# Five reorderings inside a two-block transformer kernel on one core: router work between memory-key tiles, orders in three attentions, last norm by token

## The reference, cut to what matters

```
block 1: h = x + mix(stick_breaking_attention(8 heads of 64), retention(8 heads, values of 128))
         h = h + hierarchical_moe(rms_norm(h))       # 16 experts, 2 per token, router by group
         x = rms_norm(h)
block 2: x = x + heads @ w_out,  heads = sparse latent attention (8 heads) ++ dilated attention (8 heads)
         x = x + cross_attention(rmsnorm(x), rmsnorm(mem))   # 4 heads of 256, 256 memory tokens
         x = x + square(relu(rmsnorm(x) @ w_up)) @ w_down
return rmsnorm(x)
```

## Time and profile before

| | us |
|---|---|
| median of 3 runs (lowest, highest) | 1667.63 (1666.0, 1667.67) |
| the profiled execution's own time | 1664.19 |
| its span, first to last instruction | 1662.4 |
| PE busy in the span | 1621.7 |
| mean granted TensorE clock | 0.995 |

### The profile page before, as it was taken

The page is one execution under the profiler, slowest core; times in us unless marked ns, Lnnn a source line. Parts: engine busy times, 40 slices in busy tenths (PEclk is TensorE's granted clock), DMA queues, the critical chain, the costliest instruction groups (busy, mean ns, idle before and its releaser), DMA issues.

```text
span 1662.4 us, 21089 instructions
## 1 busy us (share of the span) xinstructions
PE 1621.7 (98%) x7972; PEld 1318.5 (79%) x7972; DVE 924.4 (56%) x1116; ACT 733.0 (44%) x880; POOL 605.3 (36%) x253
## 2 busy tenths in 40 slices
PE   9999999999999999999999999999999999999996
PEld 7988888588887888888898668667877888888885
DVE  6244210682465799898967689893433552232313
ACT  5345222334344788878853332674333322221221
POOL 1412264134342243222313645663422444344441
PEclk9999999999999999999999999999999999999998
DMA  5211153212235999999954314101321222222221
GB/s 195 102 52 51 38 152 114 79 73 101 101 107 178 396 421 406 390 392 395 376 228 146 101 63 154 67 1 48 132 74 51 79 98 101 101 101 89 95 95 51
DMA packets 47139, 249.25 MB, mean 150 GB/s; under 512 B 9472, under 2 KB 10240, under 8 KB 20704
## 3 DMA queue, kind: packets, MB, share of 16 engines
q1 hardware_dynamic: 40880, 235.75, 38.2%
q0 software_dynamic: 5184, 8.40, 1.3%
q10 hardware_dynamic: 1008, 4.19, 0.6%
HBM read 236.05 MB, written 16.78 MB: 152 GB/s over the span
## 4 chain that ended last, share of the span: by engine, by line
PE 77%; issue 11%; DVE 6%; POOL 3%; ACT 2%; DMA 1%; SPq 0%; POOLq 0%; DVEq 0%; ACTq 0%
PE psum L229 22%; PE psum L231 21%; PE psum L230 21%; POOL w_lo L148 3%; PE psum L2208 2%; DVE kept_bias L2075 1%; DVE top L2074 1%; PE psum L662 1%; PE psum L2243 1%; PE psum L2231 1%; PE psum L1244 1%; PE psum L2479 1%; PE psum L681 1%; DMA raw<-in_w_dense 1%; PE psum L2499 1%
## 5 line engine op out<-in xcount | busy, mean ns | idle before, releaser
L148 POOL TENSOR_TENSOR w_lo<-raw,w_hi 128x2048 fp32r<-128x2048 f32 x91 | 419.2, 4606 | 701.6 <-ACT w_hi L142 663.3
L142 ACT ACTIVATE w_hi<-raw 128x2048 fp32r<-128x2048 f32 x96 | 183.4, 1910 | 313.8 <-PE psum L231 313.8
L229 PE MATMUL psum<-x_hi,w_hi 128*128 128x512 f32 x808 | 316.5, 392 | 1.4 <-POOL w_lo L148 0.7
L230 PE MATMUL psum<-x_lo,w_hi 128*128 128x512 f32 x808 | 314.4, 389 | 0.0
L231 PE MATMUL psum<-x_hi,w_lo 128*128 128x512 f32 x808 | 314.4, 389 | 0.0
L1262 DVE TENSOR_TENSOR moe_lo<-moe_w,moe_hi 128x2048 fp32r<-128x2048 f32 x100 | 227.7, 2290 | 31.0 <-ACT moe_hi L1252 29.9
L1252 ACT ACTIVATE moe_hi<-moe_w 128x2048 fp32r<-128x2048 f32 x100 | 190.9, 1915 | 30.1 <-PE psum L231 17.8
L229 PEld LDWEIGHTS psum<-x_hi,w_hi 128*128 128x128 f32 x808 | 151.7, 188 | 35.0 <-issue 2.0
L230 PEld LDWEIGHTS psum<-x_lo,w_hi 128*128 128x128 f32 x808 | 151.7, 188 | 31.7 <-issue 0.7
L231 PEld LDWEIGHTS psum<-x_hi,w_lo 128*128 128x128 f32 x808 | 151.7, 188 | 31.7
L434 DVE TENSOR_TENSOR res<-res,psum 128x512 f32<-128x512 f32 x56 | 38.4, 687 | 214.4 <-PE psum L231 214.4
(11 more groups left out here) (377 smaller groups left out, 2914.7 us busy)
## 6 DMA issues: line engine op xcount, KB each, us to landing
raw<-in_w_dense SPq DMA_DIRECT2D x96, 1024.0 KB, 4.8
moe_w<-in_w_moe_ahead SPq DMA_DIRECT2D x54, 1024.0 KB, 14.3
moe_w<-in_w_moe SPq DMA_DIRECT2D x48, 1024.0 KB
yrow<-expert_rows SPq DMA_DIRECT2D x8, 512.0 KB, 7.9
res<-in_x SPq DMA_DIRECT2D x4, 512.0 KB, 6.4
decay<-in_decay SPq DMA_DIRECT2D x8, 256.0 KB, 5.0
hn_rows<-hn_tok ACTq DMA_DIRECT2D x4, 512.0 KB, 7.8
out<-res SPq DMA_DIRECT2D x4, 512.0 KB, 2.7
```

What stands on the lines that cost most here:

```text
L142: act.activation(w_hi[c % RING][:, :], raw[c % RING][:, :], ACT.Copy).then_inc(hi_ready, 1)
L148: pool.tensor_tensor(w_lo[c % RING][:, :], raw[c % RING][:, :], w_hi[c % RING][:, :].bitcast(F32), ALU.subtract).then_inc(lo_ready, 1)
L229: pe.matmul(out, lh, rh, start=first, stop=False)
L230: pe.matmul(out, lh, rl, start=False, stop=False)
```

## The change

- Stick-breaking: the second `ret_v` tile of a head goes to bank 6 and waits for the low half of the last pair's values instead of the copy of the first tile; a pair's values wait until that tile is copied. On VectorE, softplus of head 0 stands before `size(1)`, and `logs_low(0)` before the copy of tile 2.
- Router: `rows(2)` stands behind tile 0 of `k_mem`, the ranks behind tile 1, `rows(3)` and the lists behind tile 2. Before, ranks, `rows(2)` and `rows(3)` stood behind tile 1 and the lists behind tile 2.
- Attention: the bias of the dilated heads is loaded before the chunks of `v_b`'s stage; the first exponential of head 0 and its table load stand between the copies of `v_b`; one chunk of the layer `out2` is rounded behind the exponentials of head 1 and subtracted by GpSimd behind all heads; VectorE normalises head 0 before it takes head 1.
- Cross attention: head 3 is turned into banks 4 and 5, right behind head 2; then come the values of both. VectorE normalises head 3 before the low halves of head 1.
- Last norm: sums of squares are made per token, as columns of 4; root and reciprocal are on 128 x 4; the reciprocal is widened by a copy and turned by 4 transposes into bank 5, and the eight products read it there. The sum of the first seven squares is reduced while the eighth is made.

```diff
@@ stick-breaking
+    SECOND_V = [tiles_of(h)[1] for h in range(HEADS) if TILES_V[h] == 2]
-            if j >= 1:
-                pe.wait_ge(bank_free, V_T + j + 4)
+            if j in SECOND_V:
+                pe.wait_ge(bank_free, V_T + j + 3)
+            elif j >= 1:
+                pe.wait_ge(bank_free, V_T + j + 4 - (j - 1 in SECOND_V))
+            pe.wait_ge(bank_free, V_T + 4 + max(j + 1 for j in SECOND_V if j < UPTO_V[min(2 * p + 1, HEADS - 1)]))
+                if j in SECOND_V and h >= 2:
+                    pe.wait_ge(y_low, h // 2)
         ret_v_out(1)
+        softplus(0)
         size(1)
-        softplus(0)
+        logs_low(0)
         ret_v_out(2)
-        logs_low(0)
@@ router
-                 tile_hooks={1: lambda: [ranks_of_tokens(), rows(2), rows(3)], 2: lists_of_experts,
+                 tile_hooks={0: lambda: rows(2), 1: ranks_of_tokens, 2: lambda: [rows(3), lists_of_experts()],
@@ attention
+                if name == "v_b":
+                    sp.wait_ge(x1_done, KT)
+                    sp.wait_ge(tables_done, 4)
+                    sp.wait_ge(bank_free, FIRST_TILE["q_rope"] + 4)
+                    sp.dma_start(dil_bias[:, :], d["dil_bias"]).then_inc(a_in, 16)
+        dense_pool(pool, "v_b", splits=1)
+            scale=tok_r12[:, j % 4:j % 4 + 1]).then_inc(bank_free, 1), splits=1,
+            tile_hooks={5: lambda: act.preload_act_table_set("exp_and_others"), 6: lambda: weigh(act, 0, 0)})
-        for h in range(2):
-            softmax(h, 0)
-            softmax(h, 1)
+        softmax(0, 0)
+        softmax(0, 1)
         normalise(0)
+        softmax(1, 0)
+        softmax(1, 1)
+        weigh(act, 1, 0)
+        weigh(act, 1, 1)
+        split_hi(act, FIRST_CHUNK["out2"] + 1, FIRST_TILE["out2"])
...
+        split_lo(pool, FIRST_CHUNK["out2"] + 1)
@@ cross attention (PE)
-        for h in range(CH_HEADS):
+        for h in range(CH_HEADS - 2):
             transposes(h)
-            if h + 2 < CH_HEADS:
-                scores(h + 2)
+            scores(h + 2)
+            values(h)
+        for h in range(CH_HEADS - 2, CH_HEADS):
+            transposes(h)
+        for h in range(CH_HEADS - 2, CH_HEADS):
             values(h)
@@ last norm
+                act.activation(last_rms[:, :], psum[:, 4, 0:TB], ACT.Sqrt, scale=1.0 / D, bias=col("eps"))\
+                   .then_inc(last_rooted, 1)
...
+        link(dve, dve.reciprocal(last_rstd[:, :], last_rms[:, :]))
+        dve.tensor_copy(last_wide[:, :, :], wide(last_rstd[:, :], [P, TB, P], 2)).then_inc(last_turned, 1)
+        dve.wait_ge(last_spread, ONCE + 1)
+        for kt in range(KT):
+            dve.scalar_tensor_tensor(out=res[:, kt, :], in0=res[:, kt, :], scalar=norm_end2.gain_of(kt),
+                                     in1=psum[:, 5, :], op0=ALU.mult, op1=ALU.mult).then_inc(n_scaled, 1)
...
-        norm_end2.pe(pe)
+        pe.wait_ge(n_added, (KT - 1) * norm_end2.u + KT - 2)
+        for q in range(TB):
+            pe.matmul(psum[:, 4, q:q + 1], norm_end2.sum[:, q * P:(q + 1) * P], ones[:, 0:1], start=(q == 0), stop=False,
+                      skip_group_check=True)
+        pe.wait_ge(n_squared, KT * (norm_end2.u + 1))
...
+        for q in range(TB):
+            mm = pe.transpose(psum[:, 5, q * P:(q + 1) * P], last_wide[:, q, :], ident[:, :])
+        mm.then_inc(last_spread, 1)
```

More of the change, by code:

```diff
@@ L176, in dense_sync, with dense_pool @@
         loop(sp, n, body)
-    def dense_pool(pool, name, after=None, halves_first=False):
+    def dense_pool(pool, name, after=None, halves_first=False, splits=2):
         n, k = turns(name)
@@ L189, in dense_pool, with dense_act @@
         loop(pool, n, body)
-    def dense_act(act, name, evac=None, hooks=None, ahead=True):
+    def dense_act(act, name, evac=None, hooks=None, ahead=True, tile_hooks=None, splits=2):
         n, k = turns(name)
@@ L204, in body @@
                     evac(act, i, j, (t0 + j) % 4)
-                if ahead or i < n - 1:
+                    if tile_hooks and j in tile_hooks:
+                        tile_hooks[j]()
+                if b < splits and (ahead or i < n - 1):
                     split_hi(act, c0 + 2 + b, t0 + per * (b + 1), i, k * per * i)
@@ L2313, in attend_vector, with weigh @@
                 low((k - 3) // 2)
+    def weigh(act, h, part):
+        b = h % 3
+        scale = (HD + 32) ** -0.5 if h < HEADS else HD ** -0.5
+        act.wait_ge(s_read, COUNTED + 2 * h + part + 1)
+        for qt in ((3,), (2, 1, 0))[part]:
+            n = P * (qt + 1)
+            ins = act.activation(score_of(h)[:, SEG[n]:SEG[n] + n], score_of(h)[:, SEG[n]:SEG[n] + n], ACT.Exp,
+                                 bias=snmax[b][:, qt:qt + 1], scale=scale, accum_out=ssum[b][:, qt:qt + 1])
+        if part:
+            ins.then_inc(s_exp, 1)
     def attend_scalar(act):
@@ L2415, in high @@
             act.activation(y_hi[:, t, :], psum[:, 2 + t % 2, :], ACT.Copy).then_inc(cv_high, 1)
-        for h in range(CH_HEADS):
+        for h in range(CH_HEADS - 2):
             copy_t(h)
-            if h + 2 < CH_HEADS:
-                exp(h + 2)
+            exp(h + 2)
             high(2 * h)
             high(2 * h + 1)
+        for h in range(CH_HEADS - 2, CH_HEADS):
+            copy_t(h)
+        for t in range(2 * CH_HEADS - 4, 2 * CH_HEADS):
+            high(t)
         residual_act(act, "o_cross", norm_mlp, root=False, gained=lambda t: norm_mlp.high_gained(act, t))
@@ L2462, in cross_stage_vector @@
                 top(h + 2)
+            if h == 1:
+                normalise(h + 2)
             low(2 * h)
             low(2 * h + 1)
-            if h + 2 < CH_HEADS:
+            if h == 0:
                 normalise(h + 2)
@@ L2520, in build @@
     f_squared, f_high, f_low, stored = sem("mlp_squared"), sem("mlp_high"), sem("mlp_low"), sem("stored")
+    last_rms, last_rstd = (at(f"last_{n}", 192 + i / 32, [P, TB]) for i, n in enumerate(("rms", "rstd")))
+    last_wide = at("last_wide", 190, [P, TB, P])
+    last_summed, last_rooted, last_turned, last_spread = lgt_done, lgt_read, first_high_done, first_low_done
+    ONCE = 1
     ORDER = [n for n, _ in LAYERS[-2 * G:]]
@@ L2591, in mlp_tensor @@
                 dense_pe(pe, name, f_hi[g % 2], f_lo[g % 2], norm=Parts(f_low, KT * g))
-        norm_end2.pe(pe)
+        pe.wait_ge(n_added, (KT - 1) * norm_end2.u + KT - 2)
[4 more added lines that the diff above has]
+        for q in range(TB):
+            mm = pe.matmul(psum[:, 4, q:q + 1], norm_end2.sq[1][:, q * P:(q + 1) * P], ones[:, 0:1], start=False, stop=True,
+                           skip_group_check=True)
+        mm.then_inc(last_summed, 1)
+        pe.wait_ge(last_turned, ONCE + 1)
+        for q in range(TB):
+            mm = pe.transpose(psum[:, 5, q * P:(q + 1) * P], last_wide[:, q, :], ident[:, :])
+        mm.then_inc(last_spread, 1)
     with nc.Block() as block:
```

58 lines of the change are left out of this document (27 added, 31 removed).

## The result

The changed kernel takes **1654.7 us** in the median (1653.0 to 1658.6) against 1667.6 before; the ratio is 0.9926, 95% interval [0.9913, 0.9939], so 12.3 us less (10.2 to 14.5; the two medians lie 12.9 apart). The forecast was 1657.2 (1654.5 to 1660.5), so the median lies 0.2 above the lower end of the range. The profiled execution of after took 1654.39 us with a span of 1652.6, which is 9.8 less than the span of before.

A forecast was written before the change was run, and what follows sets the result against it. PE was taken to bound the kernel, busy 1621.7 of 1662.4 us. Terms -4.2 - 1.2 + 0 - 2.0 - 3.0 = -10.4 took 1667.6 to 1657.2 us; range of 8 in 10, 1654.5 to 1660.5.

The forecast's parts named there:

- Stick-breaking (-4.2): Stick-breaking stage: five ret_v copy waits (-2.8) and head 0's wait (-1.4) go; bounds -3.0 and -4.3.
- Term: -2.8: Stick-breaking: PE's five waits for a ret_v tile's copy, 2.8 us in all, go with the second tile in bank 6.
- Head 0's 1.4: Stick-breaking: PE's 1.37 us stand before logs(0) goes once the softplus precedes size(1) on VectorE; -1.4.
- Router (-1.2 in the median, -1.6 against the profiled execution): Router: the lists start 1.6 us earlier despite a new 1.9 us PE stand; bounds +0.8 and -2.5.
- New order from there, all at 2.4 GHz: Router: tiles, turns and ranks reckoned from 520.5 at full clock; ranks end at 530.1, lists start at 535.7.
- the gather behind both starts no later than before: Router to experts: lists 1.6 us earlier, rows(3) copied 0.3 later; the whole shift counted into the expert stage.
- Attention (0): Attention: head 0's turns gain 1.67 us, ScalarE's moved 1.90 rounding leaves 0.3 at head 1; 0, bounds -0.5 and +1.0.
- Cross attention (-2.0): Cross attention, heads 2 and 3: two PE stands of 1.2 us become one of 0.75; bounds -1.2 and -2.4.
- last norm (-3.0): Kernel's end: last square to first product takes 3.0 us instead of 6.0; bounds -2.3 and -3.4.
- (b): Rival: clock falls in the router's new slow stretch of turns, idle time and lists, router gives nothing; about 1659.4; chance 0.17.
- (c): Rival: stick-breaking gain taken back because VectorE, not PE, sets the pace; -6.2, 1661.4; chance 0.08.
- (d): Rival: gains before the experts lost at the gather or expert weights; -5, with bad bounds -3, 1664.5; chance 0.04.

The follow-up runs named there:

- after_again: The changed kernel run a second time, unedited, for a second trace: 1655.7 us, ratio 0.9937 to the kernel before.
- after_third: The changed kernel run a third time, unedited, for a third trace: 1654.7 us, ratio 0.9923 to the kernel before.
- three_parts: Kernel before with stick-breaking, cross attention and last norm parts only; router and attention as before: 1655.0 us, ratio 0.9924.
- three_more: Changed kernel plus VectorE's k_mem subtraction behind the one-hot tables, out2's rounding 11 heads later, two closing products on GpSimd: 1656.2 us, 0.9936 to the kernel before.
- rows_early: Changed kernel with the last block's token rows turned right behind the ranks and stored earlier: 1658.3 us, one execution.
- bank_alone: Kernel before with only bank 6 for the second value tiles, VectorE's order for head 0 unchanged: 1661.0 us, one execution.
- sb_alone: Kernel before with the whole stick-breaking part alone (bank 6 and VectorE's new order for head 0): 1660.9 us, ratio 0.9965.
- rows_and_lists: Changed kernel with token rows stored early, VectorE's k_mem subtraction behind the list of tokens, out2's rounding late: 1655.4 us, ratio 0.9923 to the kernel before.
- att_alone: Kernel before with the attention part alone: 1666.1 us, ratio 0.9993.

## Why the prediction was right, and where it was not

- **The sum was right, two of its terms were not.** -10.4 was forecast. Stage by stage the traces give -5.7, -0.5 to -1.2, -0.2, -2.0 and -3.2, together -11.6 to -12.3, beside 12.3, 10.5 (after_again) and 12.8 (after_third) less from the ratios. That the median lies inside the range is partly luck. The bounds of the terms add in squares to 1.5 on the fast side and 2.7 on the slow one, not to 2 either way; with 1 for the clock the range would have started at 1654.7, where the median fell.
- **Stick-breaking (-4.2) was under-sized by 1.5.** The mechanism was right in each point: no wait of L229 for L717, no 1.4 before the first L675, no new wait. The step that failed is "PE waited five times, 2.8 us in all", and "Term: -2.8" from it. A wait is counted from the end of a 0.28 product, and its removal gives 0.8 each, 4.0 in all. Head 0's 1.4 measured 1.7 for the same reason. My bounds, -3.0 and -4.3, did not hold it.
- **Router (-1.2 in the median, -1.6 against the profiled execution).** Two steps failed, and the part's gain did not come by the way that I forecast. The first is "New order from there, all at 2.4 GHz". The tables do end 8.5 us after the start of the ranks (8.6 forecast) and PE stands 1.54 (1.9 forecast). But on the clock of before, with the shift at the router's logits taken off, the ranks began at 528.6 to 528.7 and not at 527.1, for all four traces with this order had lost 1.7 us to a fall ahead of them. So the lists came at 537.1 to 537.3, 0.1 to 0.2 earlier than in before and not 1.6. The second is "the gather behind both starts no later than before. I count the whole shift into the expert stage, whose PE never waits for data." It does wait in five of the six traces whose lists came 1.2 to 2.4 us earlier: 0.3 to 1.7 us for `moe_x`. The gather needs the stored rows too, and with the list early these were its limit. So the fall in the ranks cost before next to nothing at the end of the stage, and to avoid it gained next to nothing. What the router part gives is 0.5 to 1.2 by the end of the expert stage. Its cause is not isolated; in the traces with it PE does not wait for `moe_x`. By the runs three_parts, without it and without attention's part, is as fast as the whole.
- **Attention (0).** Right, by its mechanism: the first turns 1.8 earlier, the second 0.5, the rest 0.2. That the moved 1.90 of ScalarE was the cause is shown by three_more, in which the wait of 0.6 for its copy went.
- **Cross attention (-2.0) and last norm (-3.0).** -2.0 with a stand of 0.65 (0.75 forecast), and -3.2: the copy took 0.43 where I had assumed 0.65, the root 0.26, and the turns 0.66.
- **The level.** I let the runs' median lie 3.4 above the profiled execution on both sides. It lay 0.3 above in after. The profiled execution of before had met no fall near 1030, that of after had, which is some 1.5 of it; the rest is open, and with it how much of the 12.3 was luck of the runs.
- **Rivals.** (b) did not come in any of four traces with the 1.5 us stand. It came in rows_early, where the stand was 3.8 and the clock was at 0.50 for 7 us around it. By the Trainium skill ("TensorE: Matmul & The Clock Gate", Part 4) turns do not count as busy in the way of other products, and the traces neither refute nor settle it: in the router turns, idle time and narrow products stood together each time, and the fall near 1023 has a stand of 1.9 us ahead of it and no turns. (c) falls: in the later heads VectorE made PE wait nowhere but for the 0.4 that stood there before. (d)'s mechanism, that the gain stops at the gather, was real, but it took only the router's term: what is gained before the router moves the stores of the rows too, and passes through but for 0.5 to 0.8 (bank_alone, three_parts, sb_alone).

## What to carry to other kernels

Price a wait by the distance of the two starts around it less their usual pitch, not by the idle time between them: here 0.56 was 0.8. Where two inputs end within 0.2 us of each other (the list and the stored rows), to make one earlier is worth next to nothing, so look for everything that the consumer waits for before counting a shift into what follows. And before moving work to a new place in an engine's list, read which chain stands behind that place. Twice here the next reader got the delay: head 1's copy behind the rounding of 1.90, and in rows_early the rounding behind `rows(2)`'s copies, with VectorE's subtraction after it.

## What the runs showed of the hardware

- Falls of the clock come at a few places of an otherwise equal program, and not at each in every execution: three traces of the changed kernel had one that began at 514 to 515 each, and two of the three another that began at 1023. In traces with the router of before the one in the router was at 515, 519 or 529, or not there. Each lost 1.7 or 3.4 us. The place near 1023 stands behind a wait of 1.9 us for VectorE, which before and after_again have as well, without a fall.
- A fall costs 1.5 us or nothing, by whether PE sets the pace where it comes: near 1030 one of 1.7 moved the end by 1.5, and in the ranks one of 3.4 ended in the wait for the gather.
- The first gather took 8.5 to 9.9 us to land in every trace that shows its landing, however early it began. The next three took 4.9 to 10.1, as far as the two traces of one and the same kernel show them (after, after_again).
- GpSimd's second copy or gather took 1.8 to 3.0 us in place of 0.2 or 1.0 in six of fourteen traces: the five in which the list of tokens lay ready 1.1 us or more before the gather began, and rows_and_lists, in which it did not. In all six PE waited for gathered rows, 0.3 to 1.7 us; of the other eight traces only att_alone has such a wait, 0.4. No run shows what slows it.
